# Five levels of a triangular inverse: one burst on TensorE in place of levels between filling pieces

## The reference, cut to what matters

```python
def rwkv7_scan(r, w, k, v, a, b):
    def step(S, inp):
        r_t, w_t, k_t, v_t, a_t, b_t = inp
        sa = jnp.einsum('bhvk,bhk->bhv', S, a_t)
        S = S * w_t[:, :, None, :] + sa[..., None] * b_t[:, :, None, :] + v_t[..., None] * k_t[:, :, None, :]
        y = jnp.einsum('bhvk,bhk->bhv', S, r_t)
        return S, y
...
        gates = jax.nn.sigmoid(p_gate.astype(jnp.float32)).reshape(bsz, t, N_BRANCHES, D_MODEL)
        merged = (gates[:, :, 0] * (y_a @ w_proj_a[l]) + gates[:, :, 1] * (y_b @ w_proj_b[l])
                  + gates[:, :, 2] * (y_c @ w_proj_c[l]))
```

## Time and profile before

| | before |
|---|---|
| median of 3 runs | 1559.61 us (1559.48 to 1559.8) |
| the profiled execution | 1559.6 us, its span 1557.8 us |
| TensorE busy, whole kernel | 1529.2 us, 98% |
| VectorE, ScalarE, GpSimd busy | 69%, 27%, 8% |
| the recurrence, from its first gram to its last state product | 335.9 to 592.0 us |
| the second tile, first gram to next first gram | 399.67 to 463.36 us |

### The profile page before, as it was taken

The page is one execution under the profiler, slowest core; times in us unless marked ns, Lnnn a source line. Parts: engine busy times, 40 slices in busy tenths (PEclk is TensorE's granted clock), DMA queues, the critical chain, the costliest instruction groups (busy, mean ns, idle before and its releaser), DMA issues.

```text
span 1557.8 us, 23868 instructions
## 1 busy us (share of the span) xinstructions
PE 1529.2 (98%) x9312; PEld 1098.7 (71%) x9312; DVE 1076.8 (69%) x2049; ACT 415.7 (27%) x791; POOL 132.0 (8%) x107
## 2 busy tenths in 40 slices
PE   9999999999999999999999999999999999999997
PEld 7885544457777777776544665487858888888885
DVE  5975857874655555778599994657678887785553
ACT  3345374431101113201364764103010100000001
POOL 0020020030101100000098000000000000000000
PEclk9999999999999999999999999999999999999999
DMA  7122111111111112322122221320122222223221
GB/s 277 68 81 82 54 54 55 55 46 64 44 56 43 56 56 75 125 99 96 60 73 77 81 82 41 108 82 28 55 95 73 103 82 81 82 96 95 91 86 68
DMA packets 48720, 121.62 MB, mean 78 GB/s; under 512 B 5408, under 2 KB 19488, under 8 KB 48352
## 3 DMA queue, kind: packets, MB, share of 16 engines
q1 hardware_dynamic: 47664, 116.94, 22.3%
q10 hardware_dynamic: 720, 1.85, 0.3%
q0 software_dynamic: 224, 1.31, 0.2%
HBM read 117.98 MB, written 2.10 MB: 77 GB/s over the span
## 4 chain that ended last, share of the span: by engine, by line
PE 67%; DVE 9%; ACT 1%; issue 1%; DVEq 0%; ACTq 0%
PE bank L636 7%; PE bank L782 6%; PE vpair L1389 4%; PE opair L1389 4%; PE apair L1389 3%; PE bank L1389 3%; PE vpair L666 3%; PE opair L666 3%; PE opair L1418 2%; PE vpair L1418 2%; DVE arena L1982 2%; PE apair L666 2%; DVE arena L2677 2%; PE apair L1418 2%; PE bank L1418 2%; PE bank L666 2%
## 5 line engine op out<-in xcount | busy, mean ns | idle before, releaser
L636 PE MATMUL bank<-h,ring 128*128 128x512 f32 x560 | 254.2, 596 | 0.8 <-ACTq L1538 0.8
L636 PEld LDWEIGHTS bank<-h,ring 128*128 128x128 f32 x560 | 102.8, 190 | 115.7 <-issue 111.4
L1973 DVE TENSOR_TENSOR arena<-ring 128x512 f32<-128x512 f32 (+2 forms) x148 | 93.1, 629 | 73.1 <-DMA ring<-weights 48.0
L636 PE MATMUL bank<-arena,ring 128*128 128x512 f32 (+1 forms) x320 | 121.4, 518 | 2.1 <-ACT arena L1542 2.1
L1982 DVE SCALAR_TENSOR_TENSOR arena<-arena,cols 128x512 f32<-128x512 f32 (+1 forms) x129 | 94.8, 735 | 4.6
L636 PEld LDWEIGHTS bank<-arena,ring 128*128 128x128 f32 x320 | 57.2, 190 | 44.7 <-issue 37.9
L2958 POOL TENSOR_TENSOR arena<-arena 128x512 f32<-128x512 f32 x47 | 61.7, 1312 | 10.8 <-ACT arena L1832 7.2
L1973 DVE TENSOR_TENSOR arena<-arena 128x256 f32<-128x256 f32 (+1 forms) x114 | 57.6, 505 | 6.0 <-PE bank L993 2.2
L2963 POOL TENSOR_TENSOR h<-h,sq 128x512 f32<-128x512 f32 x2 | 2.5, 1266 | 696.5 <-ACT sq L1942 696.4
L1922 ACT ACTIVATE arena<-arena 128x512 f32<-128x512 f32 x22 | 13.9, 631 | 127.6 <-DVE arena L1982 127.6
L1973 DVE TENSOR_TENSOR arena<-ring,arena 128x512 f32<-128x512 f32 (+2 forms) x74 | 45.2, 611 | 2.5
(11 more groups left out here) (392 smaller groups left out, 3142.3 us busy)
## 6 DMA issues: line engine op xcount, KB each, us to landing
ring<-weights SPq DMA_DIRECT2D x169, 512.0 KB, 3.6
ring<-weights SPq DMA_DIRECT2D x36, 256.0 KB, 3.0
ring<-weights SPq DMA_DIRECT2D x68, 128.0 KB, 2.3
x<-xt SPq DMA_DIRECT2D x8, 512.0 KB, 8.2
ring<-weights SPq DMA_DIRECT2D x40, 64.0 KB, 2.0
out<-h SPq DMA_DIRECT2D x8, 256.0 KB, 2.8
cst<-cst_in ACTq DMA_DIRECT2D x1, 1056.0 KB, 9.7
arena<-memt SPq DMA_DIRECT2D x2, 512.0 KB, 6.1
```

Source lines behind the costliest of these rows:

```text
L636: last = mm(o[:, 0:n], weight(), src, start=c == 0, stop=c == len(srcs) - 1)
L1973: do(V.tensor_tensor(out, a, b, op), sig)
```

## The change

- The five levels run without a fill. The eight heads are two groups of four, each with a product of 8 matmuls (16 recorded) by `four_heads`: group 0 has its Y and XX in `vpair`, group 1 in `apair`, and both take turns in `opair` for XT. Each half is copied for itself: VectorE adds the identity for both Y halves and copies half 0 of XT; ScalarE copies both XX halves and half 1 of XT. `place` puts the heads of a group side by side.
- A tile's fills are 6, 6, 14, 4 and 4 units, then 4 or 8 around the state steps: 42 in place of 44. The 8 units that are left run in `finish(work)` in the last tile. The transposes of bb and k stand ahead of the burst, the product with AK behind it.
- VectorE and ScalarE read the groups by `UNITS`, the running sum of these numbers; VectorE reads none between the first mask of a tile and RB, as before, and none in the burst. `fast_weights` runs at the end of every set's fourth group (before: every second set, and for the others inside levels 3 and 4).
- Two masks of 512 elements a partition become two of 256 each.

```diff
-            return {"b": 4 * b + i, "i": 4 * (i % 2) + 2 * (i // 2) + b, "s": 4 * (b ^ (i % 2)) + i}[kind]
+            side = SIDE[kind](b, i)
+            return 4 * (i // 2) + 2 * side + (b if kind == "i" else i % 2)
...
+        FIRST_FILL, SECOND_FILL, THIRD_FILL, LEVEL_FILL, PRODUCT_FILL = 6, 6, 14, 4, 4
+
+        def state_fill(t):
+            return 4 if 0 < t < NT - 1 else 8
+
+        UNITS = [0]
+        for _t in range(NT):
+            UNITS.append(UNITS[-1] + FIRST_FILL + SECOND_FILL + THIRD_FILL + LEVEL_FILL + PRODUCT_FILL + state_fill(_t) +
+                         (4 if 0 < _t < NT - 1 else 0))
...
 
...
-                    last = [None, None]
-                    for q in range(4):
+                def four_heads(o, g, banks, lhs, rhs, rows_in, rows_out):
+
+                    for q in range(2):
...
                             for side in range(2):
...
+                                b, i = head_at(banks, 4 * g + 2 * side + q)
                                 k0, m0 = (64 * (c ^ (SIDE[rows](b, i) if rows else 0)) for rows in (rows_in, rows_out))
...
-                                                rhs(b, i)[k0:k0 + 64, :], start=True, stop=True)
...
+                def intermediate(l, g):
+
+                    n = 5 * t + l
+                    if g == 0:
+                        pe.wait_ge(ml_ready.sem, n)
+                    if l > 1:
+                        pe.wait_ge(xx_next[g].sem, 4 * t + l - 1)
+                    rows = CROSSED[l - 1]
+                    y_done[g].inc(four_heads((vpair, apair)[g], g, rows, by_bank(ML[:, n % 2]),
+                                             of(XX, CROSSED[l - 2] if l > 1 else "b"), None, rows))
+
+                def inverse(l, g):
+
+                    pe.wait_ge(y_next[g].sem, 5 * t + l)
+                    if l > 1:
+                        pe.wait_ge(xt_next[g].sem, 5 * t + l - 1)
+                    rows = CROSSED[l - 1]
+                    xx_done[g].inc(four_heads((vpair, apair)[g], g, rows, of(XT, TURNED[l - 2] if l > 1 else "b"),
+                                              of(YT, rows), rows, None))
+
+                def inverse_transposed(l, g):
+
+                    if l == 5:
+                        pe.wait_ge(y_next[g].sem, 5 * t + l)
+                        pe.wait_ge(xt_next[g].sem, 5 * t + l - 1)
+                    before = 5 * t + l - 1 + g
+                    if l > 1 or g:
+                        pe.wait_ge(xt_next[1 - g].sem, before)
+                    rows = CROSSED[l - 1]
+                    xt_done[g].inc(four_heads(opair, g, TURNED[l - 1], of(YT, rows), of(XT, TURNED[l - 2] if l > 1 else "b"),
+                                              rows, CROSSED[l]))
...
-                fill(work, 4)
+                fill(work, FIRST_FILL)
...
-                fill(work, 4)
-                for l in range(1, 6):
-                    n_ml += 1
-                    rows, next_rows, turned = CROSSED[l - 1], CROSSED[l], TURNED[l - 1]
-                    xx_kind, xt_kind = (CROSSED[l - 2], TURNED[l - 2]) if l > 1 else ("b", "b")
-                    pe.wait_ge(ml_ready.sem, n_ml)
...
-                    o = take_pair("v")
-                    for last in quad_products(o, rows, of(ML[:, n_ml % 2]), of(XX, xx_kind), None, rows):
-                        v_done.inc(last)
-                    fill(work, 2 if l < 5 else 4)
-                    pe.wait_ge(y_ready.sem, n_ml)
-                    pe.wait_ge(xt_ready.sem, n_ml + t)
-                    if l < 5:
-                        o = take_pair("a")
-                        for last in quad_products(o, rows, of(XT, xt_kind), of(YT, rows), rows, None):
-                            a_done.inc(last)
-                    o = take_pair("o")
-                    for last in quad_products(o, turned, of(YT, rows), of(XT, xt_kind), rows, next_rows):
-                        o_done.inc(last)
-                    if l < 5:
-                        fill(work, 2)
...
-                    else:
...
+                fill(work, SECOND_FILL)
+                transposed(bb)
+                transposed(k)
+                fill(work, THIRD_FILL)
+                pe.wait_ge(xx_ready.sem, t + 1)
+                pe.wait_ge(xt_first.sem, t + 1)
+                pe.wait_ge(v_read.sem, state["v"])
+                intermediate(1, 0)
+                pe.wait_ge(a_read.sem, state["a"])
+                intermediate(1, 1)
+                pe.wait_ge(o_read.sem, state["o"])
+                for l in range(1, 5):
+                    inverse(l, 0)
+                    inverse_transposed(l, 0)
+                    inverse(l, 1)
+                    intermediate(l + 1, 0)
+                    inverse_transposed(l, 1)
+                    intermediate(l + 1, 1)
+                inverse_transposed(5, 0)
+                o = take_pair("v")
+                for last in gram(o, k, r):
+                    v_done.inc(last)
+                inverse_transposed(5, 1)
+                pe.wait_ge(gram_ready.sem, 3 * t + 2)
+                pe.wait_ge(tm_ready.sem, 4 * t + 2)
+                o = take_pair("a")
+                for last in crossed_products(o, by_bank(AK), lambda b, i: vT[:, tok(2 * i + b, HD)], False, C):
+                    a_done.inc(last)
+                fill(work, LEVEL_FILL)
+                for g in range(2):
+                    pe.wait_ge(xt_next[g].sem, 5 * (t + 1))
                 pe.wait_ge(av_ready.sem, t + 1)
                 o = take_pair("a")
-                for last in quad_products(o, "b", of(XT, TURNED[4]), of(aT), "b", None, P):
+                for last in crossed_products(o, of(XT, TURNED[4]), by_bank(aT), True, P):
                     a_done.inc(last)
-                fill(work, 4)
+                fill(work, PRODUCT_FILL)
...
-                read_through(reading, GATED, 2 * GATE_PAIRS * t)
+                read_through(reading, GATED, UNITS[t] // 2)
...
                 token_rows(vT)
+                read_through(reading, GATED, (UNITS[t] + FIRST_FILL) // 2)
+                token_rows(bT)
+                token_rows(kT)
+                read_through(reading, GATED, (UNITS[t] + FIRST_FILL + SECOND_FILL + THIRD_FILL - 4) // 2)
...
+                    for g in range(2 if l < 5 else 0):
+                        act.wait_ge(xx_done[g].sem, 4 * t + l)
+                        do(fn(of_half(XX, g), (vpair, apair)[g][:, :, 0:2 * C], ACT.Copy), xx_next[g])
+                    act.wait_ge(xt_done[1].sem, 5 * t + l)
+                    do(fn(of_half(XT, 1), opair[:, :, 0:2 * C], ACT.Copy), xt_next[1])
...
-                read_through(reading, GATED, 2 * (GATE_PAIRS * t + 7))
+                read_through(reading, GATED, (UNITS[t] + FIRST_FILL + SECOND_FILL + THIRD_FILL + LEVEL_FILL) // 2)
...
-                if n_set[0] % 2 == 0 and n_set[0] < GATE_SETS:
+                if n_set[0] < GATE_SETS:
                     fast_weights("gates", n_set[0])
...
+            def added_identity(l, g):
+
+                dve.wait_ge(y_done[g].sem, 5 * t + l)
+                o = (vpair, apair)[g][:, :, 0:2 * C].rearrange("p s (q t) -> p s q t", q=2)
+                tt(of_half(YT, g), o, mask_of_pairs("ident64"), ADD, y_next[g])
...
-                read_through(reading, GATED, 2 * GATE_PAIRS * t)
+                read_through(reading, GATED, UNITS[t] // 2)
...
-                    tt(masked[:, 4 * b:4 * b + 4], part.rearrange("p (i t) -> p i t", i=4),
-                       con("levelT", 0, C).unsqueeze(1).broadcast_to([P, 4, C]), MUL, v_read)
+                    tt(of_bank(masked, b), part.rearrange("p (g m t) -> p g m t", g=2, m=2), mask_of_pairs("levelT"), MUL, v_read)
...
-                tt(by_bank(masked), chunk_product(o, 0), mask_by_bank("level0"), MUL)
+                for b in range(2):
+                    tt(of_bank(masked, b), o[:, b, 0:4 * C].rearrange("p (g m t) -> p g m t", g=2, m=2), mask_of_pairs("level0"), MUL)
...
-                read_through(reading, GATED, 2 * (GATE_PAIRS * t + 2))
+                read_through(reading, GATED, (UNITS[t] + FIRST_FILL + SECOND_FILL + THIRD_FILL - 4) // 2)
+                added_identity(1, 0)
+                added_identity(1, 1)
...
-                    read_through(reading, GATED, 2 * (GATE_PAIRS * t + 1 + l) + (l == 5))
-                    if l in (3, 4):
-                        fast_weights("gates", 2 * t + 1, (0, 1) if l == 3 else (2, 3))
...
-                    read_through(reading, GATED, 2 * (GATE_PAIRS * t + 2 + l) - 1)
-                read_through(reading, GATED, 2 * GATE_PAIRS * t + 17)
+                    dve.wait_ge(xt_done[0].sem, 5 * t + l)
+                    copy(of_half(XT, 0), opair[:, :, 0:2 * C].rearrange("p s (q t) -> p s q t", q=2), xt_next[0])
+                    if l < 5:
+                        added_identity(l + 1, 0)
+                        added_identity(l + 1, 1)
+                read_through(reading, GATED, (UNITS[t] + FIRST_FILL + SECOND_FILL + THIRD_FILL) // 2)
...
```

(6 more changed lines are left out.)

95 lines of the change are left out of this document (39 added, 56 removed).

## The result

The changed kernel takes **1594.24 us** (median of 4 runs, 1592.89 to 1596.22), the kernel before, measured beside it, 1559.69. The ratio is 1.0223, with a 95% interval of 1.0211 to 1.0235: 2.2% slower, 34.6 us. Forecast were 1575.3 us, 15.7 us more, and a range up to 1583. So the sign was right, the loss is over twice the forecast, and the time lies above the range. The profiled execution took 1594.51 us, its span 1592.7.

What follows compares the result with a forecast made beforehand. TensorE's row of instructions was taken to bound the recurrence. The terms -10.9 - 1.3 + 12.0 + 14.3 + 1.6 = +15.7 us on 1559.6 gave 1575.3 us, 1.0% slower, with a range of 1567 to 1583 us.

Steps and rivals of the forecast that it cites:

- Part 1, fewer breaks: Ahead of the products that read WU: 32 fewer cuts between fills and small products, 0.34 us each, -10.9 us.
- Part 2, the burst: The five levels without fills: TensorE idles 3.0 us a tile, +12.0 us in all, bounds 0 and +17.
- Hand-overs: In a level's loop: 0.10 us from TensorE's end to VectorE or ScalarE, 0.06 back; loop 1.96 us.
- My bound of 2.3 us a loop: Upper case for a level's loop, with 0.1 us more at three of its steps between engines; +17 us.
- The walk through one level: One level step by step: 1.41 us of TensorE's work in 1.96 us, so 0.55 us idle a level.
- Part 3, the second fill: At each tile's second fill TensorE waits until VectorE has read an earlier group: 2.3 to 4.0 us, +14.3 us in all.
- Part 4, the end of a tile: Around the state steps of the first two tiles: waits for VectorE's reads and weight sums, +1.6 us, bounds 0 and 4.
- The rival of the clock: In three second-fill waits of 4.0 us the clock falls to half: 1.8 us each, 5.4 in all, 1581 us; chance 25%.
- the full burst: In the levels without fills, hand-overs overlap more and the 12.0 us go towards 0: 1563.3 us; chance 10%.

Runs made afterwards that it cites:

- experiment 7: The changed kernel with VectorE reading early, tiles of 44 units, and two units of filling behind each of levels 1 to 4: 1560.9 us.
- experiments 2 and 4: Each against the changed kernel: six added matmuls in three of the second-fill waits, 1595.5 us; half as many instructions in the levels' products, 1585.38 us.
- experiment 10: The changed kernel with VectorE reading early, plus 32 added small matmuls in a row behind the third fill's first unit in each tile: 1576.67 us.

## Why the prediction was right or wrong

**Part 1, fewer breaks: price right.** 0.34 us forecast, 0.33 by rows, 0.30 by time.

**Part 2, the burst: this step failed,** by 59.1 - 44.4 = 14.7 us over four tiles, where I had said +12.0 with a bound of +17 and it is 59.1 - 32.4 = +26.7. Two terms of its sum are too small:
- Hand-overs, 4 x (12.36 - 11.1) = 5.0 us. The step "from VectorE's end to the TensorE start 0.06 us ... for ScalarE no row shows it; I take the same" was wrong: it is 0.15 for ScalarE, from 443.15 + 0.38 = 443.53 to 443.68 in the second tile of the changed kernel:

```profile
443.15 0.38 ACT L1819 ACTIVATE arena<-vpair 128x256 f32<-128x256 f32 x1 [8.63 <-PE vpair L1117]
```

```profile
443.68 0.46 PE L1117 MATMUL vpair<-arena 64*64 64x64 f32 x16 [0.18 <-ACT arena L1819]
```

The half product lasts 0.46 us, not 0.42; VectorE starts 0.13 behind it, ScalarE 0.12. Sum: (0.46 + 0.12 + 0.38 + 0.15) + (0.46 + 0.13 + 0.42 + 0.06) = 2.18 us, the level as measured. My bound of 2.3 us a loop held this case.
- Instructions that come late, 9.7 us. The walk through one level took for granted that TensorE always has its next instruction; no term and no rival had this. The rows of before could not show a gap, since there each level has two fills in which 16 instructions take 1.9 us. But the rate could have been worked out: a level of before (423.10 to 429.08) has 108 recorded matmuls and as many weight loads in 5.98 us, 36 a microsecond; a bare level has 192 in 2.18, 88 a microsecond; and blocks of 256 in 3.7 to 4.1 us are 62 to 69. Nothing in the trace of before showed that 88 would hold for 11 us. With four cuts (experiment 7) a burst is 1049 in 19.1 us, 55 a microsecond, and there is no gap.

**Part 3, the second fill: right.** Forecast 4.0, 4.0, 2.3, 4.0 us in tiles 1, 2, 3, 4; measured 3.85, 3.90, 2.18, 4.00.

**Part 4, the end of a tile: right in kind.** 0.4 and 0.4 us in the first tile, 0.3 in the second, 1.2 unrounded, where 1.6 in all was forecast.

**The rival of the clock was true.** I gave it 25% and 5.4 us; it came in all three long waits and cost 6.7. My reason against it ("these waits follow full work and may end in time") was worth nothing, since the row that I had named showed a fall 3.2 us after the last work, and 4.0 is longer. It belonged in the sum. Idle of 2.2 us (experiments 2 and 4) and 1.9 (experiment 10) was followed by the half clock too, so 3.2 was no safe bound either. The rule of the Trainium skill that I set beside it held in the three long waits.

The lower end of my range was a slip as well: half the way to the full burst is 1569.3 us, not 1567.

The sum with measured terms: -10.9 - 1.3 + 26.7 + 13.9 + 6.7 + 1.2 = +36.3, where 34.6 was measured. Some 0.7 of the rest are transposes: two sources side by side take 0.88 us, alone they took 0.53 each. One to two us stay open, the more as a wait costs some tenths over its row; the halves' products may save them at edges that I priced as breaks, but no run tells it.

## What to carry to other kernels

Price a wait by what it does to the row around it: the overlap that it ends (0.36 us for a row of 0.19) and, if it is near the idle after which a trace shows the clock fall, the slow work behind it. Where a change packs many small instructions together that stood between long ones, ask whether the trace shows their rate to hold anywhere; long matmuls between them are also the time in which the next instructions come. And check against a stream whose groups have to be read in order (here: 42 units instead of 44) what each reader has read when the writer comes.

## What the hardware showed that I had not expected

- TensorE can run out of instructions in straight code: gaps of 0.3 to 1.9 us, a multiple of 256 recorded instructions apart, in stretches of small matmuls; none with half the instructions for the same columns, nor with two units of filling behind each level.
- Two matmuls in a wait of 4 us kept the clock at 2.4 GHz in the profiled execution and gave back 6.7 us over three waits. One and the same wait of 2.18 us was followed by the half clock in one kernel and not in another.
